# Releasing gathered expert rows in pairs, with both output halves of a row summed side by side in one PSUM bank

## The reference

```python
# 16384 experts, 8 retrieval heads, top 16 of each; per token and head:
s_top, i_top = lax.top_k(sc, 16)                 # of 128 keys, two halves
best, pos = lax.top_k(cand, 16)                  # of the 16 x 16 sums
experts = take_along_axis(cand_idx, pos)         # 16 rows per token and head
gates = softmax(best)
act = gelu(einsum('thkd,td->thk', u_tab[experts], x))
y = einsum('thk,thkd->td', gates * act, v_tab[experts])
```

## Time and profile before

| | |
|---|---|
| median of 3 runs | 3498.65 us (3494.63 to 3506.88) |
| the profiled execution: span, first to last instruction | 3228.3 us |
| median less span (what lies around the instructions) | 270.35 us |
| PE / PEld busy | 1830.4 / 857.1 us (57% / 27%) |
| DVE busy | 2038.7 us (63%) |
| ACT busy | 705.5 us (22%) |
| POOL busy | 2058.7 us (64%) |
| moved by DMA | 1228.50 MB, mean 381 GB/s |
| mean granted TensorE clock | 0.746 |

### The profile page before, as it was taken

One profiled execution on the slowest core, in us unless ns is written; L12 is line 12 of the kernel. 1 busy time (PEld: TensorE's weight loads), 2 busy tenths in 40 slices (PEclk: granted clock), 3 DMA queues, 4 the chain that ended last, 5 costly groups with the idle time before them and its releaser, 6 DMA issues.

```text
span 3228.3 us, 31544 instructions
## 1 busy us (share of the span) xinstructions
PE 1830.4 (57%) x9976; PEld 857.1 (27%) x9976; DVE 2038.7 (63%) x5142; ACT 705.5 (22%) x1970; POOL 2058.7 (64%) x2211
## 2 busy tenths in 40 slices
PE   5998757776746776374444444444444444454543
PEld 2456543333312222141111212211121112121200
DVE  3335736666668867566666766666666666666663
ACT  2122112212214322122222211122222222211211
POOL 1233647676656656577777777777777777777774
PEclk8999778888867787686676666677767767666567
DMA  9727999999999999999999999999999999999997
GB/s 325 262 96 247 366 395 385 410 410 410 410 342 367 378 372 409 406 409 410 409 407 405 402 411 405 407 402 410 402 407 404 406 406 405 403 408 402 406 408 298
DMA packets 393188, 1228.50 MB, mean 381 GB/s; under 512 B 54563, under 2 KB 104719, under 8 KB 389678
## 3 DMA queue, kind: packets, MB, share of 16 engines
q0 software_dynamic: 305728, 1109.92, 86.8%
q1 hardware_dynamic: 46314, 75.12, 6.6%
q10 hardware_dynamic: 40980, 41.44, 3.9%
HBM read 1211.31 MB, written 16.04 MB: 380 GB/s over the span
## 4 chain that ended last, share of the span: by engine, by line
POOL 30%; DMA 28%; DVE 15%; issue 12%; PE 11%; DVEq 2%; ACTq 1%; ACT 1%; SPq 1%; POOLq 0%
DMA arena<-in_peer_u,eid 22%; POOL arena L516 15%; POOL arena L527 14%; DVE arena L1557 9%; DMA arena<-in_peer_v,eid 4%; PE PS L722 3%; PE PS L852 2%; PE PS L696 1%; DVE arena L1546 1%; ACTq L956 1%; PE PS L684 1%; PE PS L667 1%; DVE ef L1549 1%; DVE arena L1541 1%; PE PS L580 1%
## 5 line engine op out<-in xcount | busy, mean ns | idle before, releaser
L1557 DVE CUSTOM_DVE_ANT_0 arena<-arena,PS 128x1024 f32<-128x1024 f32 x1056 | 1244.3, 1216 | 795.9 <-DMA arena<-in_peer_u,eid 606.7
L852 PE MATMUL PS<-arena 128*32 128x512 f32 x4224 | 829.8, 924 | 1162.5 <-DMA arena<-in_peer_v,eid 1145.4
L516 POOL DMA_INDIRECT arena<-in_peer_u,eid x1056 | 997.8, 945 | 491.7 <-issue 294.7
L527 POOL DMA_INDIRECT arena<-in_peer_v,eid x1040 | 982.8, 945 | 476.3 <-issue 290.5
L852 PEld LDWEIGHTS PS<-arena 128*32 128x32 f32 x4224 | 165.8, 144 | 1611.4 <-issue 1604.3
L1168 ACT ACTIVATE arena<-sel,wgt 128x32 f32<-128x32 f32 x1056 | 230.7, 310 | 21.5 <-DVE wgt L1568 21.0
L684 PE MATMUL PS<-arena 128*128 128x256 f32 (+1 forms) x576 | 176.9, 463 | 14.3 <-DVE arena L1400 14.3
L822 PEld LDWEIGHTS PS<-arena 128*128 128x128 f32 x1280 | 156.3, 203 | 48.0 <-issue 48.0
L822 PE MATMUL PS<-arena 128*128 128x128 f32 x1280 | 163.7, 289 | 0.0
L1156 ACT ACTIVATE arena<-PS 128x256 f32<-128x256 f32 x42 | 16.1, 384 | 661.3 <-PE PS L833 661.3
L1151 ACT ACTIVATE arena<-PS 128x256 f32<-128x256 f32 (+1 forms) x48 | 17.1, 357 | 612.6 <-PE PS L822 612.6
(11 more groups left out here) (241 smaller groups left out, 1958.0 us busy)
## 6 DMA issues: line engine op xcount, KB each, us to landing
arena<-in_w_ada SPq DMA_DIRECT2D x24, 1024.0 KB, 8.3
arena<-in_peer_u,eid POOLq DMA_INDIRECT x1056
arena<-in_peer_v,eid POOLq DMA_INDIRECT x1056, 7.1
arena<-in_peer_wq ACTq DMA_DIRECT2D x10, 1024.0 KB, 5.6
arena<-in_peer_wq SPq DMA_DIRECT2D x4, 2048.0 KB, 37.9
arena<-in_w_in SPq DMA_DIRECT2D x14, 512.0 KB, 8.1
arena<-in_w_in ACTq DMA_DIRECT2D x14, 512.0 KB, 15.0
arena<-in_x_prompt ACTq DMA_DIRECT2D x8, 512.0 KB, 8.4
```

What stands on the lines that cost most here:

```text
L516: po.indirect_dma_start(out=Ur[:, k % RING, :], out_offset=None, in_=a["peer_u"], in_offset=bass.IndirectOffsetOnAxis(ap=eid[m % 4][:, k:k ...
L527: po.indirect_dma_start(out=Vr[:, k % RING, :], out_offset=None, in_=a["peer_v"], in_offset=bass.IndirectOffsetOnAxis(ap=eid[m % 4][:, k:k ...
L852: last = mm(PS[j * GT:(j + 1) * GT, half, :], dsel[m % 2][:, k, :], rows[:, k % RING, half * 512:(half + 1) * 512], start=m % 2 == 0 and q ...
L1557: last = ve.tensor_tensor_reduce(out=Ur[:, k % RING, :], in0=Ur[:, k % RING, :], in1=hP, scale=1.0, scalar=0.0, op0=ALU.mult, op1=ALU.add, ...
```

## The change

It sets `VB = 2`, so a V batch is two rows, there are eight per unit (`NV = 8`), and four semaphores tell of their landing instead of two. `weigh(m, b)` takes two rows: for each row first its lower then its upper half, and the column group is now 2 * half + k % 2. So one PSUM bank holds everything of a token group: partitions 0 to 63 two partial sums of the lower half, partitions 64 to 127 two of the upper. Banks 0 and 1 alternate from group to group. `take_y` is one instruction instead of two, into one of two `Yp` of half the size, and `combine` reads 64 partitions for each half instead of 128. PE's wait for the copy (`y_ev`) is for the copy of two groups earlier instead of one. PE weighs both pairs of what was a quarter one after the other, at the same place behind the pieces; POOL still issues four U rows and then four V rows. Numbers that were `NV` in the sense of four places per unit now stand as 4 or 3. The order of the gathers, the pieces and the bytes stay as they were.

```diff
-VB = 4
+VB = 2
...
-        Yp, x2b, g2v, gfv = (R(38048 + D * i, D) for i in range(4))
+        Yp = [R(38048 + 512 * i, 512) for i in range(2)]
+        x2b, g2v, gfv = (R(39072 + D * i, D) for i in range(3))
...
             for n in range(UNITS - 1):
-                for q in range(NV):
-                    if n < UNITS:
-                        gather_u(n, 2 * q)
-                        gather_u(n, 2 * q + 1)
+                for b in range(0, NV, 2):
+                    gather_u(n, b)
+                    gather_u(n, b + 1)
                     if n >= 1:
-                        gather_v(n - 1, q)
+                        gather_v(n - 1, b)
+                        gather_v(n - 1, b + 1)
...
-            for q in (2, 3):
-                po.wait_ge(s["pv_done"], (UNITS - 2) * NV + q + 1)
-                for k in range(q * VB, (q + 1) * VB):
+            for b in range(NV // 2, NV):
+                po.wait_ge(s["pv_done"], (UNITS - 2) * NV + b + 1)
+                for k in range(b * VB, (b + 1) * VB):
...
-                if q == 0 and m % 2 == 0 and m >= 2:
-                    pe.wait_ge(s["y_ev"], m // 2)
-                for half in range(2):
-                    for k in range(q * VB, (q + 1) * VB):
-                        j = k % 4
-                        last = mm(PS[j * GT:(j + 1) * GT, half, :], dsel[m % 2][:, k, :], rows[:, k % RING, half * 512:(half + 1) * 512],
-                                  start=m % 2 == 0 and q == 0, stop=m % 2 == 1 and q == NV - 1)
+                if b == 0 and m % 2 == 0 and m >= 4:
+                    pe.wait_ge(s["y_ev"], m // 2 - 1)
+                for k in range(b * VB, (b + 1) * VB):
+                    for half in range(2):
+                        j = 2 * half + k % 2
+                        last = mm(PS[j * GT:(j + 1) * GT, m // 2 % 2, :], dsel[m % 2][:, k, :], rows[:, k % RING, half * 512:(half + 1) * 512],
+                                  start=m % 2 == 0 and b == 0, stop=m % 2 == 1 and b == NV - 1)
                 last.then_inc(s["pv_done"], 1)
...
-                    last = mm(PS[p:p + GT, 2 + half, :], sel[:, :], Yp[:, half * 512:(half + 1) * 512], start=True, stop=True)
+                    last = mm(PS[p:p + GT, 2 + half, :], sel[half * 64:half * 64 + 64, :], Yp[g % 2][half * 64:half * 64 + 64, :], start=True, stop=True)
...
-                        weigh(n - 1, q)
+                        weigh(n - 1, 2 * q)
+                        weigh(n - 1, 2 * q + 1)
...
-                if g:
-                    ac.wait_ge(s["pe_cmb"], g)
+                if g >= 2:
+                    ac.wait_ge(s["pe_cmb"], g - 1)
...
-                for half in range(2):
-                    last = act_(Yp[:, half * 512:(half + 1) * 512], PS[:, half, :], ACT.Copy)
-                last.then_inc(s["y_ev"], 1)
+                act_(Yp[g % 2], PS[:, g % 2, :], ACT.Copy).then_inc(s["y_ev"], 1)
```

More of the change, by code:

```diff
@@ L534, in gather_last @@
                 po.wait_ge(s["dots_done"], (UNITS - 1) * NU + 6 + 2 * q)
-                for k in range(q * VB, (q + 1) * VB):
+                for k in range(q * RING // 2, (q + 1) * RING // 2):
                     po.indirect_dma_start(
@@ L541, in _ @@
             for n in range(UNITS - 1):
-                for q in range(NV):
-                    if n < UNITS:
-                        gather_u(n, 2 * q)
-                        gather_u(n, 2 * q + 1)
+                for b in range(0, NV, 2):
+                    gather_u(n, b)
+                    gather_u(n, b + 1)
                     if n >= 1:
-                        gather_v(n - 1, q)
[L548 to L551, removed]
+                        gather_v(n - 1, b)
+                        gather_v(n - 1, b + 1)
+            for b in range(0, NV, 2):
+                gather_u(UNITS - 1, b)
+                gather_u(UNITS - 1, b + 1)
+                if b == NV - 2:
                     gather_last(0)
-                gather_v(UNITS - 2, q)
+                gather_v(UNITS - 2, b)
+                gather_v(UNITS - 2, b + 1)
             gather_last(1)
-            for q in (2, 3):
-                po.wait_ge(s["pv_done"], (UNITS - 2) * NV + q + 1)
-                for k in range(q * VB, (q + 1) * VB):
+            for b in range(NV // 2, NV):
+                po.wait_ge(s["pv_done"], (UNITS - 2) * NV + b + 1)
+                for k in range(b * VB, (b + 1) * VB):
                     po.indirect_dma_start(
@@ L871, in _ @@
                     replicate(n // 2)
-                for q in range(NV):
+                for q in range(4):
                     for i in gap(n, q)[:1]:
@@ L880, in _ @@
                         queries(AHEAD, HU * (n - FIRST + 2) + q)
[L881 removed]
+                    if q == 3 and FIRST <= n + 2 < UNITS:
                         scores(n + 2)
[L883 removed]
+                    if q == 3 and n == FIRST - 1 or q == 1 and n >= FIRST and t < TT:
                         queries(t, h)
                     if 1 <= n <= UNITS:
[L886 removed]
+                        weigh(n - 1, 2 * q)
+                        weigh(n - 1, 2 * q + 1)
         @block.scalar
@@ L1189, in _ @@
                     gelu(n - 1)
-                left = gap(n - 1, NV - 1)
+                left = gap(n - 1, 3)
                 after_weight = [i for i in left if PIECES[i][0] in ("S", "H1", "KN", "VN", "UT")]
@@ L1202, in _ @@
                     piece(i)
-                for q in range(NV - 1):
+                for q in range(3):
                     for i in gap(n, q):
```

15 lines of the change are left out of this document (6 added, 9 removed).

## The result

| | median | runs |
|---|---|---|
| before, in the comparison | 3501.86 us | 3484.32 to 3518.47, 20 runs |
| the change | 3516.68 us | 3503.73 to 3532.82, 20 runs |

A forecast was written before the change was run, and what follows sets the result against it. The DMA engines were taken to bound the kernel from 1500 us on; release in pairs (9.8 us) and the tail (3.7 us) made 13.5 us, so 3498.65 would become 3485.2 us, range 3470 to 3504.

The forecast's parts named there:

- Sum: Whole kernel: 9.8 + 3.7 = 13.5 us less, with 270.35 us around the span unchanged, giving 3485.2 us.
- The premise: Steady part, 1500 to 3178 us: DMA engines always have something to move (share 1.02), so they bound the kernel.
- Release in pairs, 9.8 us: POOL's wait for V slots: each of seven stalls ends half a quarter sooner, the halves adding to 9.8 us.
- the seven stretches: Places before 1500 us where the DMA engines run dry; empty time of 31.1 us was to fall to some 21.
- The steady part unchanged: From 1500 us on: DMA share stays 1.02, and the distance from its start to the last gather stays the same.
- Landing in pairs, 0: PE weighs the first pair while the second lands: taken as 0, with 11 us kept for the range.
- Copy, seam and sum, 0: Shorter ACT copy, quarter's seam and 64-row combine on PE: hidden or free, 0; drains bounded at 46 us of PE time.
- The tail, 3.7 us: Last unit: 2.2 us from the last V gathers' stall, 0.96 from half a quarter, 0.5 from the copy.
- D: Rival: shorter PE bursts lower the clock between 880 and 1200 us; 15 us slower, 3514; chance 0.12.
- B: Rival: DVE and the pieces hold the next stall's end; only two stretches and the tail gain 6.5 us, 3492; chance 0.30.
- C: Rival: landing in pairs brings PE to its pieces sooner, adding 11 us for 24.5 us in all, 3474; chance 0.08.
- E: Rival: POOL finds the second pair unfinished and stands as long as before, so nothing changes; counted as part of B.

The follow-up runs named there:

- e1: The kernel before, unchanged, profiled beside its times on a chip like the first profile's: 3229.11 us against 3228.98 for its twin, ratio 1.0002.
- under load: Copies from HBM to HBM added from unit 24 on, on slow chips; with the uneven kind before took 3516.30 us, landing in pairs with release in fours 3535.08.
- both in fours: The change with release and landing both joined to four rows again, except in the last unit, against before on a fast chip: 3226.95 us, 0.9989.
- the layout alone: Before with only the new sums (one bank per token group, one copy, combine over 64 partitions), batches of four: 3228.65 and 3228.12 us, both 0.9999.
- uneven load: Eight 24 KB copies per unit added from unit 24, two slow chips: before 3517.66 and 3516.30 us, the change 3524.92 and 3523.55.
- even load: Three 512 KB copies per unit added from unit 24, meant for all DMA engines, slow chip: before 3520.88 us, the change 3521.29.

## Why the prediction was wrong, by its own steps

**The step that failed** is the premise on what bounds the kernel, taken for the timed runs from a profile that was not of them; and in "Sum": "with the 270.35 us around it, which I take as unchanged". The difference of 270.35 us is not around the span. The profiled execution of before ran in one condition (span 3228.3 us, the whole time some 2 us more, as e1 shows with 3226.2 and 3228.16), the three timed runs in another (3495 to 3507). Every row that the prediction read is of the first condition, and the comparison was of the second. A number beside the rows should have raised the question: 8% of the time outside the span, where the profile after has 2 us.

**The premise** "from 1500 to 3178 us ... there is always something for them to move" holds on three chips (406 GB/s, share 1.02) and fails on those of the other kind (361 to 366, 0.95 to 0.97). The term that was put at 0 behind this cover is landing in pairs, which cost 21.9 us there by itself, under load. And release in pairs, costed as a gain of 9.8 us, brought none: by itself it was +10.4 ± 11.5. In place of 13.5 us less, the comparison shows 14 us more. How the two halves make up the 14 us isn't shown: on a slow chip without load only the whole change was run.

**Release in pairs, 9.8 us.** On the fast chips: unit 24 comes 1420.1 - 1414.0 = 6.1 us sooner in the first run of the change and 7.2 in the second, 7.9 and 7.6 with the release alone, and the release alone is worth 7 to 8 us of time. (The two profiles of before differ by 1.7 us at that unit.) The empty time of the seven stretches fell by 31.1 - 23.6 = 7.5 us. The mechanism is the predicted one, with about three quarters of its size; the "some 21 us" left were 23.6. The step that took the sum of all seven halves was too much: at the third stretch a piece that waited for DVE held PE's quarter back. POOL's waits for PE, 181.6 us in before, are 111.8 and 113.3: they fell by 70, ten times what shows in the time. Half of that is the release (140.9 and 142.9 with it alone), half the landing (147.8 and 143.4), and the time followed the release.

**The steady part unchanged.** From unit 30 to 65 it is 1463.6 us and 1464.2: right on those chips.

**Landing in pairs, 0.** 0.6 to 2.4 us faster on fast chips, no more than both in fours, so right. On the slow chip under load it is the costly half: +21.9 us by itself. PE's busy time tells of its work: 1950.7 us after and 1952.9 for the change with load, 1891.7 for before with load. In its steady part POOL waits for PE's slots for 260 us, so such work may no longer be hidden; how much of the 61 us comes through is not told apart.

**Copy, seam and sum, 0.** Right on fast chips: the layout alone was twice 0.9999, and the seam, with both in fours, cost nothing either (0.9989). The prediction's bound for a drain was 46 us of PE time; PE's busy time with the layout alone is 1803.7 and 1811.1 us, against 1830.4 and 1825.5 in before. The Trainium skill, *TensorEngine Tiling (Array Packing)*, section Key Properties, says that a change of tiling mode drains TensorE. The traces show no such cost where PE is hidden, and no run had the layout alone on a slow chip, so there it stays open.

**The tail, 3.7 us.** From the last `eid` to the end of the span: 89.4 and 89.5 us before, 89.2 and 87.8 in the change. But the layout alone, without pairs, has 89.7 and 87.9, so no gain in the tail is shown. The stall of 2.49 us did vanish, but the step "the last four V gathers" went by POOL's issues, and rows asked for sooner took longer to come. In the kernel before the last quarter began 8.4 us after the last gather's issue at 3204.71; here the last pair began 10.65 us after it (3205.10 against 3194.45). The 0.96 us for half a quarter did not come either: the last pair took 1.93 us, as the quarter had. What was there is the shorter copy, 0.60 us against 1.08. That rows wait longer in the queues is the very cover that the prediction had named for the steady part.

**The rivals.** D put the loss on the clock between 880 and 1200 us, deciding under 0.67. There the clock of the change on the first such chip is 0.74, as before:

```profile
880.00:1200.00 320.00, 201.34 (x810) 86.01 (x806) 242.55 (x584) 93.78 (x283) 193.19 (x200) 0.74 0.97 373
```

So D did not happen where it was put. Over the whole span the mean clock did fall on the fast chips, 0.745 to 0.718 (landing in pairs alone does it; the release alone leaves 0.737), and the kernel was faster all the same. The Trainium skill, *TensorE: Matmul & The Clock Gate*, on oscillation, describes bursts between waits for DMA that run at the lower clock. The traces agree as to the clock, and show no price of it where PE is hidden. On the slow chip under load PE is busy for 61 us more in the change, at a mean clock of 0.708 against 0.728 in before; but the clock can't be all, since release in pairs alone kept 0.726 there and was not faster than before. B's 6.5 us is near what the release brought, but partly by luck: the stretches behind the second gained too (the last of the seven stalls ends at 1169.43 us, against 1176.97 and 1175.48 in the two profiles of before), and its 3.7 us of tail didn't come. Its mechanism, the pieces holding the next stall's end, is seen at the third stretch. C is off: the 11 us of landings didn't come. E is refuted by the 2.24 us. That the time of comparison had other bounds was no rival of mine, and it should have been the first.

**Left open.** What makes a chip slow (see the last section). Why release in pairs, which asks for rows sooner, does not gain where POOL waits for slots throughout; the three changed kernels with uneven load on the second chip had 50 to 140 us more of idle time ahead of the weights on DVE than before with the same load, but under the even load the change had 15 us less than before, so this is a poor witness. The share of the layout on slow chips is open too.

A version that beats both kernels was not found: on fast chips release in pairs with landing in fours is as good as the change to within 2 us, on the slow chips, with load, nothing was faster than before.

## What to carry to other kernels

Lay the profiled execution's time beside the timed runs before reading a row of it; where they differ by more than what can lie around a span, the rows are of another condition, and each cost "hidden behind the DMA engines" needs a second price for the case that they aren't full. Waking the gathers sooner paid 7 to 8 us here, in stretches in which the DMA engines ran dry behind that wait on fast chips; on the slow chips it paid nothing. In the steady part of the fast chips and in the tail a stall removed did not shorten the time. Letting PE begin on half of a batch was free on fast chips, where its work is hidden, and cost 21.9 ± 11.1 us on a slow one under load, so release and landing are worth setting and measuring separately.

## What was not expected of the hardware

The times of one kernel fall into two groups. On three chips before took 3228.5 to 3229.8 us, on two 3481 and 3484, and the whole comparison lay at 3502. Each chip was seen at one time only, so whether it is the chip or the hour isn't told apart; nor is it on record whether other cores of the chip were at work at the time, which is the first rival to test. The bytes are the same, the mean packet of a gather takes longer, and the 16 engines aren't kept busy. Part 3 of the page, the gathers' queue (packets, MB, share of 16 engines' span), of the change on a fast chip and then of the profile after, the same kernel:

```profile
q0 software_dynamic: 305728, 1109.92, 87.0%
```

```profile
q0 software_dynamic: 305728, 1109.92, 83.1%
```

83.1% of 3514.7 us is 2921 us, 87.0% of 3219.9 is 2801: the same packets took 4% more of the engines' time, while the span grew by 9%. The rest is time in which the engines had nothing of this queue. On the slow chips engines also stand for nothing that the trace shows. The groups view has "issue" ahead of PE's weighing for 259.7 us of 1600 in before with load and 262.8 in the change, and none in before on the fast chip in the same stretch (its 841.5 us of idle time all end with a landing):

```profile
L852 PE MATMUL PS<-arena 128*32 128x512 f32 x2448 | 515.0, 986 | 841.5 <-DMA arena<-in_peer_v,eid 841.5
```

```profile
L865 PE MATMUL PS<-arena 128*32 128x512 f32 x2192 | 488.4, 980 | 876.6 <-DMA arena<-in_peer_v,eid 451.2 <-issue 259.7 <-remote 83.9
```

```profile
L868 PE MATMUL PS<-arena 128*32 128x512 f32 x2161 | 523.3, 932 | 753.4 <-issue 262.8 <-DMA arena<-in_peer_v,eid 260.4 <-ACT arena L1185 149.7
```

Of PE alone that would be a weak sign: on fast chips too the weighing has 113.4 and 114.2 us of it in the change, and 131.6 in the layout alone, without a loss of time. On DVE it marks the slow chips: the waits view has 2.7 us of "issue" in that stretch for before and for the change on the first fast chips, 142 in the profile after, and 246 and 284 in the two with load. Whether late landings, late instructions or lost records are behind that, no run tells.
